# The gate projections of the first layer's attention at every third unit

## The reference

```python
h = rmsnorm(x, norm_mix_pre[i])
z = h @ w_in[i]
xr, gr, q, kc, vc, ksl, vsl, kw, vw, g_nsa, gm_rnn, gm_attn = jnp.split(z, IN_SPLITS, axis=-1)
y_rnn = rg_lru(causal_conv(xr, ...), ...) * jax.nn.gelu(gr)
y_attn = nsa(q, kc_c, vc_c, ksl, vsl, kw, vw, g_nsa, slopes)   # 16 heads of 64, softmax in each branch
y = jax.nn.sigmoid(gm_rnn) * y_rnn + jax.nn.sigmoid(gm_attn) * y_attn
x = x + rmsnorm(y @ w_out[i], norm_mix_post[i])
```

## Time and profile before

| | |
|---|---|
| median of 3 runs | 2311.96 us |
| lowest and highest | 2299.86 and 2323.68 us |
| profiled execution | 2335.96 us, span 2334.2 us |
| PE busy | 2070.3 us (89%) |
| DVE, ACT, POOL busy | 1328.9 us (57%), 809.3 us (35%), 576.9 us (25%) |
| mean granted TensorE clock | 0.945 |
| DMA, mean over the span | 307 GB/s; 413 to 422 GB/s in most of the last 25 of the 40 slices |

### The profile page before, as it was taken

The page is one execution under the profiler, slowest core; times in us unless marked ns, Lnnn a source line. Parts: engine busy times, 40 slices in busy tenths (PEclk is TensorE's granted clock), DMA queues, the critical chain, the costliest instruction groups (busy, mean ns, idle before and its releaser), DMA issues. The chain is left out here.

```text
span 2334.2 us, 24093 instructions
## 1 busy us (share of the span) xinstructions
PE 2070.3 (89%) x7860; PEld 1274.9 (55%) x7860; DVE 1328.9 (57%) x2941; ACT 809.3 (35%) x2272; POOL 576.9 (25%) x530
## 2 busy tenths in 40 slices
PE   7999999899999849997789999887999989788776
PEld 6898876788656436643335664443666455332222
DVE  2612442899513245788874454488546458955444
ACT  1413331444312213433333353333336334433332
POOL 0000000000000013434444234333323433443332
PEclk9889968899999969998989999999999999999999
DMA  7432202455434229999999999999999999999997
GB/s 263 150 126 92 81 27 70 157 187 191 153 135 163 81 107 422 421 413 413 417 413 421 421 421 421 421 416 408 381 421 421 420 421 419 384 420 422 421 421 316
DMA packets 99607, 716.56 MB, mean 307 GB/s; under 512 B 11040, under 2 KB 11168, under 8 KB 13472
## 3 DMA queue, kind: packets, MB, share of 16 engines
q0 software_dynamic: 75584, 545.09, 56.7%
q1 hardware_dynamic: 23616, 168.94, 19.3%
q10 hardware_dynamic: 288, 1.05, 0.1%
HBM read 713.99 MB, written 1.05 MB: 306 GB/s over the span
## 5 line engine op out<-in xcount | busy, mean ns | idle before, releaser
L1085 PE MATMUL bank<-arena 128*128 128x512 f32 x2048 | 991.2, 622 | 199.7 <-ACT arena L1550 198.2
L1797 DVE SCALAR_TENSOR_TENSOR arena<-arena,x_tok 128x1024 f32<-128x1024 f32 x512 | 619.6, 1226 | 512.3 <-DMA arena<-peer_uv,arena 508.4
L1648 POOL DMA_INDIRECT arena<-peer_uv,arena x512 | 560.4, 1095 | 917.9 <-PE bank L1085 809.9
L1085 PEld LDWEIGHTS bank<-arena 128*128 128x128 f32 x2048 | 377.0, 196 | 701.2 <-ACT arena L1550 356.4
L755 PE MATMUL bank<-xT,weight_ring 128*128 128x128 f32 (+2 forms) x2544 | 439.2, 330 | 5.4 <-DVE xT L1672 4.0
L755 PEld LDWEIGHTS bank<-xT,weight_ring 128*128 128x128 f32 (+1 forms) x2544 | 392.1, 192 | 87.0 <-issue 41.4
L1543 ACT ACTIVATE arena<-arena 128x1 f32<-128x1 f32 x512 | 103.4, 202 | 891.3 <-DVE arena L1797 890.4
L1537 ACT ACTIVATE arena<-const_tile,arena 128x128 f32<-128x128 f32 x512 | 198.1, 387 | 6.1 <-DVE arena L1789 6.1
L1550 ACT ACTIVATE arena<-arena 128x128 f32<-128x128 f32 x512 | 198.0, 387 | 0.6
L1285 ACT ACTIVATE arena<-bank 128x512 f32<-128x512 f32 (+6 forms) x164 | 78.8, 493 | 275.9 <-PE bank L755 275.8
L755 PE MATMUL bank<-arena 128*128 128x128 f32 (+10 forms) x888 | 165.5, 341 | 9.9 <-DVE arena L2160 4.9
(11 more groups left out here) (203 smaller groups left out, 1355.5 us busy)
## 6 DMA issues: line engine op xcount, KB each, us to landing
weight_ring<-weights SPq DMA_DIRECT2D x159, 1024.0 KB
arena<-peer_uv,arena POOLq DMA_INDIRECT x512
row_ring<-rows_in POOLq DMA_DIRECT2D x10, 512.0 KB, 5.4
const_tile<-consts POOLq DMA_DIRECT2D x1, 1849.0 KB, 8.1
x_tok<-x_in SPq DMA_DIRECT2D x2, 512.0 KB, 4.6
memT<-memT_in POOLq DMA_DIRECT2D x1, 1024.0 KB, 10.9
row_ring<-rows_in ACTq DMA_DIRECT2D x2, 512.0 KB, 14.7
x_out<-x_tok SPq DMA_DIRECT2D x2, 512.0 KB, 5.4
```

Source lines behind the costliest of these rows:

```text
L1085: ins = pe.matmul(b[:, :], diag[n % DIAGS], gbuf[n % GBUF][:, 1, h * 512:(h + 1) * 512], start=n % P == 0, stop=n % P == P - 1)
L1648: pool.indirect_dma_start(gbuf[n % GBUF].rearrange("p a d -> p (a d)"), None, peer_uv, bass.IndirectOffsetOnAxis(ap=expert[t][:, s:s + 1]. ...
L1797: dve.scalar_tensor_tensor(u, u, 1.0, x[:, t, :], ALU.mult, ALU.mult, accum_out=hdot[:, s:s + 1])\
```

## The change

One line of the order changes: gate 3 + n stands at step 3n in place of the whole part of 5n/2.

```diff
--- before.py
+++ after.py
@@ -65,7 +65,7 @@
     for u in range(len(UNITS) + 3):
         if u < len(UNITS):
             order.append(("score", u))
-        order += [("gate", NZ0 + n) for n in range(NZ - NZ0) if n * 5 // 2 == u]
+        order += [("gate", NZ0 + n) for n in range(NZ - NZ0) if 3 * n == u]
         if 0 <= u - 2 < len(UNITS):
             order.append(("turn", u - 2))
         if 0 <= u - 3 < len(UNITS):
```

## The result

| | kernel before | changed kernel |
|---|---|---|
| median of 20 runs | 2323.32 us | 2329.68 us |
| lowest and highest | 2298.06 and 2335.75 us | 2323.91 and 2342.51 us |
| profiled execution | 2335.96 us | 2340.00 us |

A forecast was written before the change was run, and what follows sets the result against it. PE was taken to bound the attention, so only waits and clock count: -9.6 + 7.9 + 4.6 = +2.9 us, which on the median of 2311.96 us gave 2315 us, range 2300 to 2330 us.

The forecast's parts named there:

- Part (a): Attention tail: units 21 to 24 come ahead of the last gate, at the high clock, giving back 9.6 us.
- Part (b): Behind gate 7: an uncovered wait of 3.2 us, then low clock costing 2.7 and 2.0 us; 7.9 us lost.
- the three jobs: Turn, value and score between gate 7's wait and gate 8, at the low clock: 2.7 us lost.
- Part (c): Gate 4 moves to unit 3: PE waits 2.6 us at turn 0, perhaps at low clock after; 4.6 us lost.
- The sum of +2.9 us: Net change in the attention: -9.6 + 7.9 + 4.6 us; this near-zero trade had a chance of 0.80.
- all 214 records: Matmul records behind the last gate's wait in the kernel before, all said to run at the low clock.
- How the numbers follow: Step that weighed the cases and took the runs' 12 us to either side of the median as measurement spread.
- the tail at full clock: Rival: the clock does not fall behind gate 11, the last ten units run fast; 24 us less, 2291 us; chance 0.06.
- the chain from POOL's product over DVE's small one to PE's wait: Behind the last gate: POOL multiplies for 4.51 us, DVE's tiny product takes 4.02 us, PE waits 3.24 us.
- The drain of about 1.38 us: Per ACT table load, would lengthen gate 7's wait by up to 2.8 us; left out of the sum.

The follow-up runs named there:

- tail_only: Kernel before with only the last two gates later (gates at steps 0, 2, 5, 7, 10, 12, 15, 20, 24); ratio 0.9974 to the kernel before.
- gate4_back: Changed kernel with gate 4 back at step 2, the other gates as changed; median 2321.23 us, ratio 1.0004 to the kernel before.
- extra3: Changed kernel with three repeated products in the score of unit 22, same result; median 2326.44 us, profiled run 2309.09 us.
- split_gate7: Changed kernel with POOL's first product alone cut into eight; median of 12 runs 2320.87 us.
- extra6: Changed kernel with six repeated products in the score of unit 22, same result; median 2325.89 us.
- split_before: Kernel before with each of POOL's two products on 128x2048 elements cut into eight of 128x256; ratio 0.9898 to the kernel before.

## Why the prediction was wrong

Part (a), 9.6 us: right for a run whose tail is at the low clock. tail_only measured 9.7 us, and the gaps held the clock. In a run whose clock comes back early the four units run at the high clock already, and there is nothing to give back.

Part (b), 7.9 us: right in kind and near in size. The wait was 3.24 us, the three jobs lost 2.6 and gate 8 lost 2.7, 8.5 us together; in gate4_back, by the same rows, 3.2, 2.6 and 1.6, 7.4 us.

Part (c), 4.6 us: right. The wait was 2.52 us, and the clock did fall: 4.2 us in the first trace, 5.6 in the second (2.52, gate 4 with 8.82 in place of 7.17 us, and turn and score with 3.19 in place of 1.74 us). Of the eight traces that have this wait the clock held in two, extra3 and split_gate7, where it cost the 2.5 us alone. The prediction's "between 2.6 and 6.5" is what runs do by turns.

The sum of +2.9 us stands against 3.3 us in the profiled stretch, and 3.3 us between the means of nine and two traces. That the two profiled executions differ by as little was luck in one thing: both fell on the same level, the uppermost.

Two readings in it are slightly off. The slices at the end of the attention read 9, 6 and 8, not 9, 6 and 9. And the clock doesn't stay low for all 214 records: it was back at 372.8 us, 2.6 us before their end.

What failed is the step "How the numbers follow". It took the 12 us to either side of the median for a spread that a measurement carries, and moved the median by the sum. The spread was a set of levels, and the sum was made for the levels of the long tail alone. The term that it put at nothing without a reason is what the change does to the runs on the low levels. 39 of 144 runs of the kernel before lie 24 us below the level of their fellows, and none of 32 of the changed kernel.

By size 0.27 x 24 = 6.5 us of the difference of the means, 10.6 us, are this loss, 3.3 the sum of the attention, and about 1 the early stretch of 60 columns, which was low in 11 of 32 runs against 37 of 144 (0.09 x 12). In the twenty runs against twenty of the result the difference of the means is 15.0 us: 7 of 20 on the low levels, 8.4 us; 3.3; and 9 against 4 early stretches at the low clock, 3.0 us, for which no run shows a cause in the change. Of the 6.5 us a part would be gone even at an unchanged share: an early return saves 24 us with fourteen units behind the last gate and only some 14 with ten. But the share has fallen too, from 39 in 144 to none in 32.

The clock as a thing that differs between runs did stand in the prediction, but only as a rival for the changed kernel (the tail at full clock, 2291 us); that runs of the kernel before have it already, and that the change could take it away, did not. The waits and the clock were right for the run that was traced; which share of the runs that run stands for was not asked. The run times shown, 2299.86, 2311.96 and 2323.68 us, at equal steps of 12, were a hint.

The base was off for the same reason. The median of three runs, 2311.96 us, was one run of each of three levels; twenty gave 2323.32 us. Of the 14.7 us between the forecast of 2315 and the measured 2329.68 us, 11.4 lie there. That the measured median still lies inside the range, at its edge, and within 1% of the kernel before is owed to the width that was given for noise, not to the step.

Why the changed kernel never shows the early return stays open, and so does why gate4_back, tail_only and split_gate7 show it in at most one run of 36. tail_only has no low stretch in the attention ahead of the tail that the kernel before has not, so the waits at gate 4 and behind gate 7 aren't needed for the loss. extra3 and extra6 bring lower runs back (6 of 24) with the waits in place, by 0.7 and 1.3 us of work between them and the last gate, so the timing there seems to matter; the moment of the fall alone doesn't decide. That the 2300 us runs of the kernel before are the early return is inferred from extra3, from their size (the 23.4 us above; 28 us would be all of it, as split_before shows) and from their mean clock, 0.960 to 0.966 against 0.947 to 0.957 on the main level; no trace of such a run was caught. That the runs near 2311 us are the same with the early stretch at the low clock is inferred from the levels alone.

Two steps of the working were confirmed by split_before: the chain from POOL's product over DVE's small one to PE's wait, and the clock that falls for this wait alone. The drain of about 1.38 us that the Trainium skill (ScalarE: Activation LUTs, on what a table load costs) adds to a table load is not in this trace either: in split_before the load of 1.28 us begins at 299.33 us and the exponential behind it at 300.62. On the point of change that differs from run to run (TensorE: Matmul & The Clock Gate, Part 1) the traces agree with the Trainium skill: behind the last gate it came between 1.3 and 3.1 us into the same wait of the two kernels.

## What to carry to other kernels

A wait on TensorE is worth more than its length if the clock falls with it: 3.24 us of waiting cost some 28 us here. Where a tiny DVE instruction is held up beside one long POOL instruction, cutting the long one into pieces lets it through: eight pieces gave the 28 us back. Where run times stand at equal steps, a trace is of one level: find what makes the levels before adding a sum to the median, compare level with level, and count how often each occurs, since a change can go along with other shares. Extra gates to keep the engine dense were not needed; small products held the clock once no wait stood between them.

## What the runs showed of the hardware

The granted clock, once lost, mostly stayed lost for long under small products although PE was busy: 58 to 68 us at 0.50 in all nine traces of the kernel before, while the same kind of work held it at 1.00 through the 14 units of split_before. It can come back in the same work after 3.4 us (extra3) or only after 44 us (extra6), with the same fall 3.4 us into the wait. The wait of 3.23 or 3.24 us dropped the clock in every trace that has it, the one of 2.52 us in six of eight. Products of 60 columns between 96 and 128 us ran at 1.00 in seven and at 0.56 in two traces of the unchanged kernel. A DVE product of 128x2 elements takes 0.16 us alone, 4.02 us beside one POOL product of 4.51 us, and 0.23 and 0.50 us beside eight of 0.7 us.
